# Next token group's slabs loaded by the sync engine, first gate pieces through the turned weights' places, output's first splits made in attend

## The reference

```
h = rmsnorm(x, g_norm);  z = h @ w_in          # 7424 columns = 58 chunks of 128
qa ka va ga | qb kb vb gb | qc gc | gm = split(z)
A: rope, sliding window of 128 with sinks, 8 query heads on 2 key heads
B: stick-breaking attention over all earlier keys, 8 heads of 64
C: attention on 256 memory rows (rmsnorm(mem) @ w_mem_kv), 4 heads of 128
y_i = (o_i * silu(g_i)) @ w_br_i
x + (sum_i sigmoid(gm_i) * y_i) @ w_out, then a final rmsnorm
```

## Time and profile before

| | |
|---|---|
| runs of the kernel (3) | 3017.08 to 3020.94 us, median 3019.62 us |
| the profiled execution | 3014.48 us, of which the span from first to last instruction is 3012.7 us |
| busy: PE, DVE, POOL, ACT | 2876.6, 1510.9, 1165.8, 1005.1 us |
| mean granted TensorE clock | 0.984 |
| HBM read and written | 359.08 and 123.60 MB |

### The profile page before, as it was taken

The page is one execution under the profiler, slowest core; times in us unless marked ns, Lnnn a source line. Parts: engine busy times, 40 slices in busy tenths (PEclk is TensorE's granted clock), DMA queues, the critical chain, the costliest instruction groups (busy, mean ns, idle before and its releaser), DMA issues.

```text
span 3012.7 us, 49757 instructions
## 1 busy us (share of the span) xinstructions
PE 2876.6 (95%) x20331; PEld 2377.8 (79%) x20331; DVE 1510.9 (50%) x2147; ACT 1005.1 (33%) x1843; POOL 1165.8 (39%) x1006
## 2 busy tenths in 40 slices
PE   6999999999998999989998999989998998999997
PEld 5888888888887788867776777767776777899886
DVE  7332221100014777566676677667765786444432
ACT  5541111111113444334443444334443664111221
POOL 5432331111114454445453555445454565444100
PEclk9999999999999999999999999999999999999999
DMA  7533332222235544655557554664457547756542
GB/s 230 190 144 119 135 124 65 78 69 70 71 125 172 171 151 168 225 191 182 167 186 253 166 175 168 216 227 163 148 180 190 176 137 222 218 148 220 176 143 94
DMA packets 381570, 485.95 MB, mean 161 GB/s; under 512 B 27840, under 2 KB 241472, under 8 KB 380960
## 3 DMA queue, kind: packets, MB, share of 16 engines
q1 hardware_dynamic: 339744, 359.13, 38.1%
q0 software_dynamic: 34688, 111.05, 10.0%
q10 hardware_dynamic: 6912, 12.59, 1.2%
HBM read 359.08 MB, written 123.60 MB: 160 GB/s over the span
## 4 chain that ended last, share of the span: by engine, by line
PE 87%; DVE 5%; issue 3%; DMA 2%; ACT 2%; ACTq 1%; POOL 0%; SPq 0%; DVEq 0%; POOLq 0%
PE prj_bank L391 9%; PE prj_bank L393 9%; PE prj_bank L392 9%; PE stk_g_bank L835 6%; PE stk_g_bank L837 6%; PE stk_g_bank L836 6%; PE stk_turn_bank L907 5%; PE stk_o_bank L924 4%; PE stk_z L880 4%; PE stk_z L862 4%; PE out_y L2010 3%; PE out_y L2011 3%; PE out_y L2012 3%; PE stk_z L893 2%; PE stk_o_bank L933 2%
## 5 line engine op out<-in xcount | busy, mean ns | idle before, releaser
L391 PE MATMUL prj_bank<-hidden_hi,w_hi 128*128 128x512 f32 (+2 forms) x1360 | 490.0, 360 | 0.0
L1141 POOL TENSOR_TENSOR stk_beta<-stk_beta,stk_left 128x1024 f32<-128x1024 f32 (+4 forms) x160 | 275.8, 1724 | 549.2 <-DVE stk_left L1053 549.2
L393 PE MATMUL prj_bank<-hidden_hi,w_lo 128*128 128x512 f32 (+2 forms) x1360 | 486.2, 358 | 0.0
L392 PE MATMUL prj_bank<-hidden_lo,w_hi 128*128 128x512 f32 (+2 forms) x1360 | 485.9, 357 | 0.0
L835 PE MATMUL stk_g_bank<-hidden_hi,w_hi 128*128 128x512 f32 (+2 forms) x928 | 350.5, 378 | 4.6 <-ACT stk_g_out L967 4.6
L837 PE MATMUL stk_g_bank<-hidden_hi,w_lo 128*128 128x512 f32 (+2 forms) x928 | 336.0, 362 | 0.0
L836 PE MATMUL stk_g_bank<-hidden_lo,w_hi 128*128 128x512 f32 (+2 forms) x928 | 334.9, 361 | 0.0
L393 PEld LDWEIGHTS prj_bank<-hidden_hi,w_lo 128*128 128x128 f32 x1360 | 256.1, 188 | 32.4
L391 PEld LDWEIGHTS prj_bank<-hidden_hi,w_hi 128*128 128x128 f32 x1360 | 256.3, 188 | 31.2
L392 PEld LDWEIGHTS prj_bank<-hidden_lo,w_hi 128*128 128x128 f32 x1360 | 256.4, 189 | 31.0
L1053 DVE TENSOR_TENSOR_SCAN stk_left<-stk_rest,stk_left 128x513 f32<-128x513 f32 x192 | 247.9, 1331 | 11.3 <-ACT stk_rest L997 11.1
(11 more groups left out here) (275 smaller groups left out, 5537.1 us busy)
## 6 DMA issues: line engine op xcount, KB each, us to landing
w_raw<-in_w_in SPq DMA_DIRECT2D x130, 512.0 KB, 3.8
stk_kd<-in_cache_sb_k SPq DMA_DIRECT2D x64, 1024.0 KB, 5.5
stk_vd<-in_cache_sb_v SPq DMA_DIRECT2D x64, 1024.0 KB, 7.6
scratch_zT<-stk_g_out POOLq DMA_DIRECT2D x72, 256.0 KB, 2.7
out_gate<-scratch_zT SPq DMA_DIRECT2D x24, 768.0 KB, 4.9
scratch_zT<-prj_z POOLq DMA_DIRECT2D x48, 256.0 KB, 2.3
out_u_raw<-scratch_uT SPq DMA_DIRECT2D x9, 1024.0 KB, 11.0
nrm_x<-in_x_prompt SPq DMA_DIRECT2D x16, 512.0 KB, 3.7
```

What stands on the lines that cost most here:

```text
L391: pe.matmul(out, w_hi[u][:, k, :], hi[:, k, :], start=k == 0, stop=False)
L392: pe.matmul(out, w_hi[u][:, k, :], lo[:, k, :], start=False, stop=False)
L393: last = pe.matmul(out, w_lo[u][:, k, :], hi[:, k, :], start=False, stop=k == KC - 1)
L1141: pool.tensor_tensor(bt, bt, left[prompts.index(n) % 2][:, :, 1:keys + 1], ALU.mult).then_inc(a_done, 1)
```

## The change

Nine edits, in the order of the phases:

- normalize: `empty(c)` moves on ScalarE one step later and ahead of `round_hi`; `copy_rows` on VectorE likewise.
- project makes 30 chunks; the four QC chunks (queries of branch C) become filler of stick: `filler` has 28 chunks, `gpieces` 140 pieces, with 16 more splits of weights than before (28 chunks in each of 4 groups, for 24). They are copied, not passed through the sigmoid.
- stick: the 6 lead pieces leave through the four halves of `a_t` (where the turned weights of attention go later), each with a semaphore of its own; VectorE's first `copy_a` waits until they are stored.
- stick: `load_hidden` moves from ScalarE (16 DMAs of 256 KB) to SP (8 DMAs of 512 KB), ahead of the step's other loads; SP waits there for the group's last piece.
- stick: `load_early` also waits for the stores of the queries of group 0, of lead and later pieces.
- stick to attend: `KEEP` is 1, and this last piece is made in attend, at its step 2; the first splits of attend's keys and queries move into stick's last steps, VectorE's two memsets to attend's step 2.
- attend to output: `first_dead` lets the first output weights load when the last sample keys are turned; ScalarE makes the first `w_hi` and the first four `u_hi` in attend's last three score steps, VectorE the four `u_lo` in the steps behind them, GpSimd the first `w_lo` at step N.
- output: the second weights' split comes ahead of the last four `u` tiles.
- SBUF tensors of attend and output stand in another order, so that these overlaps are allowed.

```diff
             for T in range(len(tiles) + 2):
                 if T <= LAST:
                     square(T)
+                if T - 2 in product_at:
+                    empty(product_at[T - 2])
                 if 1 <= T <= LAST + 1:
                     round_hi(T - 1)
-                if T - 1 in product_at:
-                    empty(product_at[T - 1])
...
-              + [(c, "copy") for c in range(QC, QC + 4)] + [(c, "silu") for g in (GA, GB, GC) for c in range(g, g + 4)])
+              + [(c, "silu") for g in (GA, GB, GC) for c in range(g, g + 4)])
...
-    GC_N = 24
+    filler = list(range(GM, GM + 24)) + list(range(QC, QC + 4))
+    GC_N = len(filler)
...
-    LEAD, KEEP = 6, 2
+    LEAD, KEEP = 6, 1
...
+        def out_of(p):
+            return a_t[p % 2][:, p // 2 % 2, :] if p < LEAD else g_out
...
+            def load_hidden(v):
+                sp.wait_ge(g_summed, turn_over[v - 1] + 1)
+                for k in range(0, KC, 2):
+                    for h in (0, 1):
+                        sp.dma_start(f32(hid_last[h][:, k:k + 2, 0:512]),
+                                     d["hid"][h, token_groups[v], k:k + 2, :, :].rearrange("k p n -> p k n")).then_inc(slab_loaded[k // 2], 16)
...
             for s in range(N + LAG_O):
+                if s - 1 in ended_at and ended_at[s - 1] in turn_over:
+                    load_hidden(turn_over.index(ended_at[s - 1]) + 1)
                 if s - 1 in ended_at and ended_at[s - 1] in w_last and w_last.index(ended_at[s - 1]) + 3 < WN:
                     load_w(w_last.index(ended_at[s - 1]) + 3)
...
             def empty(p):
                 w = gpieces[p][3]
                 act.wait_ge(g_summed, p + 1)
-                wait(act, g_stored, 16 * p)
-                act.activation(g_out[:, 0:w], bank_of(p)[:, 0:w], ACT.Sigmoid).then_inc(g_emptied, 1)
+                if p < LEAD:
+                    wait(act, lead_stored[p % 4], 16 * (p // 4))
+                else:
+                    wait(act, g_stored, 16 * (p - LEAD))
+                act.activation(out_of(p)[:, 0:w], bank_of(p)[:, 0:w], ACT.Sigmoid if gpieces[p][1] < 24 else ACT.Copy).then_inc(g_emptied, 1)
...
-                if p in turn_over:
-                    load_hidden(turn_over.index(p) + 1)
...
+                if n == 0:
+                    leads_stored(dve)
...
             for s in range(N + LAG_O):
                 if s == LAG_O:
                     pe.wait_ge(*stk["g_emptied"])
+                if s == 2:
+                    stk["tail"]["tensor"](*stk["last"])
...
+                if s >= N - 3:
+                    output["scalar"](act, s - N + 3)
...
+                if s >= N:
+                    output["vector"](dve, s - N)
...
+                if s == N:
+                    output["gpsimd"](pool)
...
+        def ahead_act(act, x):
+            if x == 0:
+                round_weights(act, 0)
+            if x in (1, 2):
+                round_u(act, 0, 2 * x - 2)
+                round_u(act, 0, 2 * x - 1)
...
-            sp.wait_ge(*att["sample_turned"])
+            sp.wait_ge(*att["first_dead"])
             weights(0)
```

More of the change, by code:

```diff
@@ L706, in first_tile, with leads_stored, piece_stored @@
             return place[:, :].rearrange("p (c n) -> p c n", c=8)[:, :, 0:P]
+        def leads_stored(eng):
+            for i in range(4):
+                eng.wait_ge(lead_stored[i], 16 * len(range(i, LEAD, 4)))
+        def piece_stored(eng, p):
+            eng.wait_ge(g_stored, 16 * (p - LEAD + 1))
         def tokens(p):
@@ L1121, in store_gates @@
                 pool.wait_ge(g_emptied, p + 1)
-                pool.dma_start(d["zT"][GM + c, :, tokens(p)], g_out[:, 0:w]).then_inc(g_stored, 16)
+                pool.dma_start(d["zT"][filler[c], :, tokens(p)], out_of(p)[:, 0:w]).then_inc(lead_stored[p % 4] if p < LEAD else g_stored, 16)
             def rest_w(x):
@@ L1543, in _ @@
             for s in range(N + LAG_O):
+                if s == 2:
+                    stk["tail"]["scalar"](stk["last"][0])
                 if s - LAG_T in by_act:
@@ L1693, in _ @@
             for s in range(N + LAG_O + 1):
+                if s == 2:
+                    stk["tail"]["gpsimd"](stk["last"][0])
+                if s == N:
+                    output["gpsimd"](pool)
                 if s in round_at:
@@ L1769, in w_out, with round_weights, round_u, rest_u @@
             return w[:, c, 0:KC, :]
+        def round_weights(act, c):
+            act.wait_ge(w_loaded[c % 2], 64 * (c // 2) + 64)
+            act.activation(w_hi[:, c, :, :], w_raw[c % 2][:, :, :], ACT.Copy).then_inc(w_hi_done, 1)
+        def round_u(act, g, k):
+            width = GROUP[g][1]
+            if k % 4 == 0:
+                act.wait_ge(u_loaded[k // 4], 16 * g + 16)
+                if g:
+                    act.wait_ge(summed, count(g - 1, KC - 1, k // 4))
+            act.activation(u_hi[:, k, 0:width], u_raw[:, k, 0:width], ACT.Copy).then_inc(u_hi_done, 1)
+        def rest_u(dve, g, k):
+            width = GROUP[g][1]
+            dve.wait_ge(u_hi_done, 12 * g + k + 1)
+            dve.tensor_tensor(u_lo[k][:, 0:width], u_raw[:, k, 0:width], f32(u_hi[:, k, 0:width]), ALU.subtract).then_inc(u_lo_done, 1)
+        def ahead_act(act, x):
[4 more added lines that the diff above has]
+                round_u(act, 0, 2 * x - 1)
+        def ahead_dve(dve, x):
+            if x in (1, 2):
+                rest_u(dve, 0, 2 * x - 2)
+                rest_u(dve, 0, 2 * x - 1)
+        def ahead_pool(pool):
+            pool.wait_ge(w_hi_done, 1)
+            pool.tensor_tensor(w_lo[:, 0, :, :], w_raw[0][:, :, :], f32(w_hi[:, 0, :, :]), ALU.subtract).then_inc(w_first_done, 1)
+        stack.close()
+        att_bank, att = phase_attend(nc, block, d, ident, places, stk, dict(scalar=ahead_act, vector=ahead_dve, gpsimd=ahead_pool))
         @block.sync
@@ L1854, in _ @@
         def _(act):
-            def weights(c):
-                act.wait_ge(w_loaded[c % 2], 64 * (c // 2) + 64)
-                act.activation(w_hi[:, c, :, :], w_raw[c % 2][:, :, :], ACT.Copy).then_inc(w_hi_done, 1)
             def out_weights(c):
@@ L1944, in _ @@
                     s = c % 2
-                    if g == 0 and c + 1 < KC:
+                    if g == 0 and 1 <= c < KC - 1:
                         weights(c + 1)
@@ L1954, in _ @@
                         if c == KC - 1 and g < LAST:
-                            rest_u(g + 1, i)
+                            for k in range(4 * i, 4 * i + 4):
+                                rest_u(dve, g + 1, k)
                     if g == LAST:
@@ L2070, in build @@
             stk_bank, stk = phase_stick(nc, block, d, ident, last, w_raw[0], w_hi, w_lo, places, prj, prj_bank)
-        att_bank, att = phase_attend(nc, block, d, ident, places, stk)
-        out_bank = phase_output(nc, block, d, first, stk, att)
+        att_bank, out_bank = phase_output(nc, block, d, ident, first, places, stk)
     for bank in (stk_bank, att_bank, out_bank):
```

146 lines of the change are left out of this document (75 added, 71 removed).

## The result

The changed kernel took **2964.97 us** (median of 4 runs, 2959.02 to 2966.27) against 3019.05 us for the kernel before (4 runs, 3017.08 to 3020.94): a ratio of 0.982, with a 95% interval of 0.9808 to 0.9832. The forecast was 2962 us, with a range of 2940 to 2984. The profiled execution took 2965.99 us with a span of 2964.2, which is 48.5 us less than the span of before; the medians differ by 54 us.

A forecast was written before the change was run, and what follows sets the result against it. The prediction took TensorE to set the time nearly everywhere, through its waits and half-speed stretches. Its terms, -7 - 10 - 24 - 11 - 8 + 2 = -58 us, added to the 3019.62 us median gave 2962 us, range 2940 to 2984.

The forecast's parts named there:

- Normalize, -7: Normalize: TensorE's waits for scaled tiles shrink down to VectorE's floor; -7 us, bounds -3 and -9.
- The lead, -10: Lead of stick: with four places the stores drop out and TensorE's gap ends earlier; -10 us, -6 to -13.
- about 925: End of the lead: time in us at which the weights' chain of loads, splits and sigmoids would end, against 933.33.
- Turn-overs, -24: Stick's turn-overs: slab loads issued on SP free ScalarE's sigmoids from 8.05 us of issuing; -24 us, -12 to -33.
- (a): Turn-overs and both attend boundaries: the next bound, VectorE or exponentials, takes most back; -38 us, 2982 us; chance 0.14.
- The floors give 10.7, 8.1 and 7.2 us, 26 together: Three turn-overs: savings if each window shrinks to VectorE's 19.9 to 20.2 us of work.
- Stick to attend, -11: Stick's end to attend's fifth scores: moved gate pieces and an earlier chain to exponentials; -11 us, -5 to -15.
- Attend to output, -8: Attend's last matmul to output: first weights and four u tiles split earlier; -8 us, -4 to -10.
- Moved chunks, +2: Project to stick: four chunks cost +4.5, covered waits return 3 to 4, splits +1; +2 us, -3 to +8.
- (b): Lead, turn-overs and boundaries: full-speed clock and filler give the upper bounds; -80 us, 2940 us; chance 0.12.
- (c): Turn-overs: slabs on SP's queue delay cached keys and values; mild about 2985 us, chance 0.09; full 3043, 0.03.
- the edits cancel: Whole kernel: the edits give no net change; chance 0.02.

The follow-up runs named there:

- the undone kernels: Changed kernel with one edit taken back each: normalize order 2972.6 us, lead's places 2966.6, slab issue 2983.1, QC chunks 2965.6, output splits 2972.4.
- 12.7 undone: Changed kernel with ScalarE issuing the 16 slab DMAs again: 2983.1 us; its three turn-over windows took 90.8 us instead of 78.1.
- tail_piece_first: Changed kernel with the last gate piece ahead of attend's first scores instead of behind the second, memsets left at step 2: 2964.2 us.
- undone 7.5: Changed kernel with output's first weights and first four u tiles split behind attend's loops again, loads staying early: 2972.4 us, +7.5.
- the undone kernel: Changed kernel with the four QC chunks back in project and 24 filler chunks in stick: 2965.6 us.
- the relieved kernel: Changed kernel with ScalarE making all four key copies and the second weights copy in the 15 pause steps behind the turn-overs: 2947.9 us.
- the relief gave in all: Changed kernel with ScalarE making all four key copies and the second weights copy in every step of stick: 2938.4 us, 26.6 less.

## Why the prediction was right, and where its steps were off

Five of the six terms came within 2 us of what the traces show, and the sixth, the turn-overs, was 11 us too large. In the profiled executions the sum is -48.5, so the total was 9.5 us too large there. That the median of 2965 us lies only 3 us from the forecast's 2962 is in part luck: the medians differ by 5.6 us more than the two profiled executions do, and no trace shows where. The range of 2940 to 2984 us would have held with -48.5 as well. Term by term, forecast against the traces and the undone kernels:

- **Normalize, -7:** -6.2 in the traces, 7.7 in the medians. Right, floor included: the 2.3 us gaps became mostly 1.4 to 1.7 us, once 3.3 (not under 1 us, as the forecast had it), and VectorE is nearly full.
- **The lead, -10:** -11.4 in place, right in size. The mechanism was half right: the four places give 2 to 5 us, and the filler piece that the new shares put between the second and third scores gives much of the rest. The chain of "with four places the stores drop out, and the weights' chain is what ends last" came as forecast: it gave "about 925", 25.9 us after the lead's start at 899.1, and the sigmoids began 25.9 us after it (825.21 against 799.32), behind a split that had waited for its load. What the prediction did not look up is that the first filler piece would stand in the gap, so that TensorE never stopped. The wait in `copy_a(0)` cost 1.0 us at most.
- **Turn-overs, -24:** -12.9 in the traces, 12.7 undone. This is the step that failed, and the failure is the one that case (a) priced, three times 4 us. "The floors give 10.7, 8.1 and 7.2 us, 26 together" took VectorE's 20 us as a length that the window can reach. (Two of its windows also began 2.4 us late; over the full ones of 30.6, 30.6 and 29.8 us the same rule would have given 30 us, still farther off.) In the second window, of 24.5 us, VectorE is busy for 20.3: it stands still for the first 2.1 us and four more times for 0.3 to 0.8 us, each time waiting for TensorE, and TensorE waits for it four times. The 20.3 us themselves hold waiting too: the gate product of 1.48 us ahead of the key copy takes 0.29 us where GpSimd does nothing beside it (last section). Where VectorE was relieved, the windows of 19.2 and 19.3 us stood 1.5 us above TensorE's own 17.7 and 17.8. A floor is not a forecast when the bound engine must itself wait.
- **Stick to attend, -11:** -14.3 at the boundary, +2.3 in attend behind it (5.3 less the 3.0 that the output splits cost), so -12.0. Right. The cover of 5.64 us is 5.6 in its place, but tail_piece_first, which has the piece ahead of the chain, takes no longer: the traces leave 2.6 us of it and the medians none.
- **Attend to output, -8:** -9.8 and +3.0 for the splits within attend, -6.8; undone 7.5. Right, and the small delay that the prediction named is 1 to 4 us, not "a little".
- **Moved chunks, +2:** +0.8 in the traces, -0.6 by the median of the undone kernel. Right: +3.7 of the +4.5, and -2.9 of the -3 to -4.

The sum of these is -48.5 in the profiled executions and -54 in the medians, against -58.

**The rivals.** (a) was right at the turn-overs and wrong at the boundaries. (b) needed VectorE to be no bound; the relieved kernel shows what it is worth then, 2948 us. (c) is refuted, with 12 us of slack beside the slabs themselves. The waits for VectorE's key copies were to be 1 to 3 us; the longest at the three turn-overs are 3.9, 3.4 and 3.4. That the edits cancel is refuted.

The Trainium skill (DMA: Bandwidth & Descriptors, Issuing engines are not separate DMA queues) says that another issuing engine saves only issue time. The slabs agree: what came back is ScalarE's stall of 7 to 8 us, of which 4 us a turn-over reached the end, and a slab DMA, now of twice the size, lands 8.0 to 10.0 us after its issue (medians at the first turn-over), where it took 6.0 to 8.0.

## What to carry to other kernels

When a stall is removed, look at the engine that waits next in the same window, and expect to land between its busy time and the old window; here half of the distance was won, and a relief of 11 us on that engine was worth 17.6 us in the windows where the edit itself was worth 12.7. Steps without filler are where the second-busiest engine shows most (17 of the 27 us that the relief gave in all), so work that can go to an idle engine should go there first. An engine's busy time can hold waiting for a neighbour, so look at how long the same instruction takes elsewhere before you take it for a floor. A piece of covering work gives its full length where it stands, and part or all of it can be lost a few steps later; price both.

## What the runs showed of the hardware

- Three windows, each with one wait of 3.4 to 3.9 us and some shorter ones, ran at a granted clock of 0.88, 0.93 and 0.93, and at 1.00 when the waits were under 1 us. The half-speed work was 4.9 of the 17.6 us that the relief gained. The clock fell behind all three long waits, but not at the same moment. Behind the wait of 3.91 us the transposes took 1.97 us instead of 1.09, at once; behind that of 3.38 us in the second window they took 1.09, and the eight matmuls after them 2.18, where the relieved kernel took 1.46. The granted clock was 1.00 over 1578.4 to 1579.5 us and 0.50 over 1579.9 to 1582.0. So look some us past a wait for its price.
- VectorE's gate product of 128x128 elements took between 0.29 and 2.86 us, median 1.55, over 64 times. The Trainium skill (SBUF — State Buffer, Who interferes with whom) says that VectorE and GpSimd share a port pair as an exclusive lock. The trace agrees: in 49 of the 64 a computing instruction of GpSimd was under way when the product began, and it ended 0.15 to 0.16 us behind that instruction's end; in 14 none was, and it took 0.29 us; the last, of 2.86 us, ended 0.15 us behind a split that began 0.3 us after it. One pair of each kind:

```profile
1576.07 1.54 POOL L1167 TENSOR_TENSOR stk_beta<-stk_beta,stk_left 128x766 f32<-128x766 f32 x1 [1.75 <-DVE stk_left L1074]
1576.28 1.48 DVE L1105 TENSOR_TENSOR stk_gate<-stk_o_sum,stk_gate 128x128 f32<-128x128 f32 x1
...
1523.89 0.63 POOL L1167 TENSOR_TENSOR stk_beta<-stk_beta,stk_left 128x254 f32<-128x254 f32 x1 [0.68 <-DVE stk_left L1074]
1524.68 0.29 DVE L1105 TENSOR_TENSOR stk_gate<-stk_o_sum,stk_gate 128x128 f32<-128x128 f32 x1
```

  A product of 1.48 us stands ahead of the late key copy in each of the three turn-overs. No run moves GpSimd's multiply out of its way, so what that would give at the turn-overs isn't shown.
- SP issued the 8 slabs in 4.4 to 5.1 us, and at the second turn-over the two loads behind them then stood 1.6 and 5.9 us in issue (1.2 and 4.3 at the first turn-over, 0.5 and 6.5 at the third). Nothing waited for that here.
- With the new order the end of normalize scatters over 73.3 to 80.8 us in twelve profiled kernels that run the same instructions there; the two with the old order ended it at 85.7 and 86.4. The cause stays open, and two traces can't say whether the old order scatters less.
